# Second attention layer of a streaming encoder: where its cached keys are turned, and in which order two small products run

## The reference

```python
def fox_attend(q, k, v, cq, ck, qpos, kpos):
    s = jnp.einsum('bqhd,bkhd->bhqk', q, k) * (FOX_HEAD_DIM ** -0.5)
    s = s + swapaxes(cq, 1, 2)[:, :, :, None] - swapaxes(ck, 1, 2)[:, :, None, :]
    s = jnp.where(kpos[None, :] <= qpos[:, None], s, -jnp.inf)
    return jnp.einsum('bhqk,bkhd->bqhd', softmax(s, axis=-1), v)

def swiglu_ffn(x, w_in, w_out):
    a, u = jnp.split(x @ w_in, 2, axis=-1)
    return (jax.nn.silu(a) * u) @ w_out
```

## Time and profile before

| | |
|---|---|
| time of three runs, median (lowest to highest) | 1886.13 us (1880.18 to 1888.01) |
| profiled execution, span from first to last instruction | 1885.1 us |
| TensorE busy | 1849.9 us (98%) |
| VectorE, ScalarE, GpSimd busy | 983.0, 722.0, 225.9 us |
| HBM read, written | 243.19 MB, 13.19 MB |
| first and second attention steps | about 118 to 190 and 1487 to 1568 us |
| up product of the third layer's FFN | about 1105 to 1285 us |

### The profile page before, as it was taken

How to read it: one execution, slowest core, us unless ns; L and a number is a source line. 1 busy time by engine, 2 the same in 40 slices (tenths; PEclk the granted TensorE clock), 3 DMA queues, 4 the chain that set the end, 5 groups by cost and what they waited for, 6 DMA issues and landing times.

```text
span 1885.1 us, 29064 instructions
## 1 busy us (share of the span) xinstructions
PE 1849.9 (98%) x12004; PEld 1642.4 (87%) x12004; DVE 983.0 (52%) x1569; ACT 722.0 (38%) x1144; POOL 225.9 (12%) x357
## 2 busy tenths in 40 slices
PE   8999999999999999999999999999999999999998
PEld 8777799998888887799998899998897777999986
DVE  4557653443567778743443664443465576543434
ACT  4246443333255454333332343333242463433321
POOL 3114070000011222230000100000031230000000
PEclk9999999999999999999999999999999999999999
DMA  7357254433353433444433434433364562444332
GB/s 246 128 203 229 81 160 123 129 129 123 117 164 105 125 116 104 118 139 125 124 134 123 146 101 125 132 124 125 110 206 150 200 221 90 137 132 124 128 129 79
DMA packets 179171, 259.38 MB, mean 138 GB/s; under 512 B 14717, under 2 KB 122349, under 8 KB 179040
## 3 DMA queue, kind: packets, MB, share of 16 engines
q1 hardware_dynamic: 161184, 197.18, 32.3%
q0 software_dynamic: 17856, 60.35, 9.9%
HBM read 243.19 MB, written 13.19 MB: 136 GB/s over the span
## 4 chain that ended last, share of the span: by engine, by line
PE 90%; DVE 4%; ACT 3%; issue 1%; DMA 1%; SPq 0%; DVEq 0%; ACTq 0%
PE ps L1605 14%; PE ps L1607 14%; PE ps L1606 14%; PE ps L1617 11%; PE ps L1615 11%; PE ps L1616 11%; PE ps L1833 1%; PE ps L1951 1%; PE ps L1938 1%; PE ps L1638 1%; PE ps L1888 1%; PE ps L1671 1%; DVE w_lo L785 1%; PE ps L1908 1%; PE ps L1673 1%
## 5 line engine op out<-in xcount | busy, mean ns | idle before, releaser
L785 DVE TENSOR_TENSOR w_lo<-w_raw,w_hi 128x1024 fp32r<-128x1024 f32 x370 | 452.1, 1228 | 709.1 <-ACT w_hi L439 707.9
L439 ACT ACTIVATE w_hi<-w_raw 128x1024 fp32r<-128x1024 f32 x370 | 389.3, 1059 | 803.5 <-DMA w_raw<-in_w_ffn_in_dram 363.1
L1605 PE MATMUL ps<-xT_hi,w_hi 128*128 128x384 f32 x1568 | 528.4, 337 | 2.5 <-issue 1.4
L1607 PE MATMUL ps<-xT_hi,w_lo 128*128 128x384 f32 x1568 | 527.0, 336 | 0.0
L1606 PE MATMUL ps<-xT_lo,w_hi 128*128 128x384 f32 x1568 | 526.9, 336 | 0.0
L1605 PEld LDWEIGHTS ps<-xT_hi,w_hi 128*128 128x128 f32 x1568 | 294.8, 188 | 5.2 <-issue 5.1
L1606 PEld LDWEIGHTS ps<-xT_lo,w_hi 128*128 128x128 f32 x1568 | 294.8, 188 | 0.1
L1607 PEld LDWEIGHTS ps<-xT_hi,w_lo 128*128 128x128 f32 x1568 | 294.8, 188 | 0.0
L1617 PE MATMUL ps<-w_hi,hT_lo 128*128 128x512 f32 x528 | 210.6, 399 | 0.0
L1616 PE MATMUL ps<-w_lo,hT_hi 128*128 128x512 f32 x528 | 208.1, 394 | 0.0
L1615 PE MATMUL ps<-w_hi,hT_hi 128*128 128x512 f32 x528 | 207.4, 393 | 0.0
(11 more groups left out here) (329 smaller groups left out, 2021.8 us busy)
## 6 DMA issues: line engine op xcount, KB each, us to landing
w_raw<-in_w_ffn_in_dram SPq DMA_DIRECT2D x352, 256.0 KB, 3.2
w_raw<-in_w_ffn_out_dram SPq DMA_DIRECT2D x176, 256.0 KB, 2.9
w_raw<-in_w_fox_in_dram SPq DMA_DIRECT2D x96, 256.0 KB, 2.9
k_c<-in_cache_fox_k_dram POOLq DMA_DIRECT2D x32, 512.0 KB, 5.3
v_c<-in_cache_fox_v_dram POOLq DMA_DIRECT2D x32, 512.0 KB, 4.0
w_raw<-in_w_hgrn_in_dram SPq DMA_DIRECT2D x64, 256.0 KB, 2.9
w_raw<-in_w_fox_out_dram SPq DMA_DIRECT2D x32, 256.0 KB, 2.9
out_dram<-kv_tok POOLq DMA_DIRECT2D x4, 1024.0 KB, 5.0
```

The lines of the kernel that those rows point to most:

```text
L439: nc.scalar.activation(w_hi[:, slot, :], w_raw[:, slot, :], ACT.Copy).then_inc(hi_ready, 1)
L785: V.tensor_tensor(w_lo[:, slot, :], w_raw[:, slot, :], w_hi[:, slot, :].bitcast(F32), ALU.subtract).then_inc(lo_ready, 1)
L1605: mm(out, w_hi[:, slot, cols], x_hi[:, k, :], start=k == 0, stop=False, skip_group_check=True)
L1607: last = mm(out, w_lo[:, slot, cols], x_hi[:, k, :], start=False, stop=k == KD - 1, skip_group_check=True)
```

## The change

For the layer i = 3 (`AHEAD`) the cached keys are no longer turned by TensorE in the attention loop. In the FFN of layer 2, GpSimd loads them as `k_nat`, four streams and 256 columns at a time (1 MB in 1 KB pieces, `cached_keys`). VectorE turns them by eight transposes of 128x256 in blocks of 32x32, each writing every eighth word of `k_turn` (`turn_keys_ahead`, behind `hT_lo` of chunks 1 to 8). SP stores the result to a DRAM tensor `keys_t`, in four DMAs of 32 partitions (`store_turned`, behind the weight loads of chunks 3 to 10). In layer 3 SP loads `k_t` from it, 512 KB in 1 KB pieces for each half stream, three slots: the first three before the last projection chunk, the others in the loop, between the sixth and the seventh unit of the output product (`turned_keys`). GpSimd puts the 16 new keys into `k_t` (`new_keys`); SP's keys replace its `load_k`. `ktc`, L605, L928 and L929 are left out in this layer, and `s_keys` with them.

Also in layer 3 alone: the bias product goes ahead of `s_out` and of the pairs (`s_bias`, it starts the accumulation, the pairs end it); `s_fold` moves into the middle of `p_scores` and `p_out`; `folded_hi` on ScalarE goes behind the exponential and `folded_lo` on VectorE behind the scaling of the prompt's probabilities; and GpSimd's third `v_c` load waits for `c_lo`. Semaphores of other layers are used again. The core of the diff, in which `b0`, `cols` and the new memory places are cut:

```diff
@@ sync
+            def turned_keys(i, first, end):
+                f = FOX[i]
+                for n in range(first, end):
+                    b, hf = n // 2, n % 2
+                    if n < KV:
+                        sync.wait_ge(*at(KEYS["stored"], 64 * DB))
+                        sync.wait_ge(unit_used, START[i]["mix"])
+                    else:
+                        sync.wait_ge(*at(f["s_scores"], n - KV + 1))
+                    sync.dma_start(k_t[:, n % KV, :, 0:PAST], keys_t[b, hf * WCOLS:(hf + 1) * WCOLS, :].rearrange(
+                        "(g p) k -> p g k", p=P)).then_inc(KEYS[f"in{n % KV}"][0], 16)
+            def store_turned(n):
...
+                sync.wait_ge(*at(KEYS["turned"], n + 1))
+                for r in range(4):
+                    sync.dma_start(keys_t[b0 + r, cols, :].rearrange("(c d) k -> d c k", d=32),
+                                   k_turn[32 * r:32 * r + 32, :, :, :].rearrange("d c k a -> d c (k a)")).then_inc(KEYS["stored"][0], 16)
...
+                    if i == AHEAD:
+                        chunks(w_fox_in[j], s["mix"], 6, 0, 5 * CU)
+                        turned_keys(i, 0, KV)
+                        chunks(w_fox_in[j], s["mix"], 6, 5 * CU)
+                        chunks(w_fox_out[j], s["out"], 2, 0, RING)
+                        turned_keys(i, KV, 2 * DB)
+                        chunks(w_fox_out[j], s["out"], 2, RING)
...
+                    if i + 1 == AHEAD and 3 <= c < CF:
+                        store_turned(c - 3)
@@ scalar, fox
                     if 1 <= n <= HEADS:
                         act.wait_ge(*at(f["s_nmax"], n))
...
+                    if 2 <= n <= HEADS + 1 and i == AHEAD:
+                        folded_hi(n - 2)
+                    if 1 <= n <= HEADS:
                         act.wait_ge(*at(f["s_pT"], n))
...
-                    if 1 <= n < HEADS:
+                    if 1 <= n < HEADS and i != AHEAD:
                         act.wait_ge(*at(f["ktr"], n + 1))
@@ vector, ffn and fox
+                    if i + 1 == AHEAD and 1 <= c <= DB:
+                        turn_keys_ahead(c - 1)
+            def turn_keys_ahead(n):
+                dve.wait_ge(*at(KEYS["loaded"], 16 * (n + 1)))
+                if n:
+                    dve.wait_ge(*at(KEYS["stored"], 64 * n))
+                for a in range(TWIN):
+                    ins = V.transpose(k_turn[:, :, :, a], k_nat[:, a, :])
+                ins.then_inc(KEYS["turned"][0], 1)
...
                         ins.then_inc(f["scaled"][0], 1)
+                    if 2 <= n <= HEADS + 1 and i == AHEAD:
+                        folded_lo(n - 2)
...
-                        if n:
+                        if n and i != AHEAD:
                             key_sides(n, KT_BANKS + 1)
@@ gpsimd
+                if i == AHEAD:
+                    pool.wait_ge(*at(f["c_lo"], 3))
+                else:
+                    pool.wait_ge(unit_used, m0 + 12)
+                    load_k(KV - 1)
                 load_v(KV - 1)
...
+                    if n < 2 * DB and i == AHEAD:
+                        pool.wait_ge(*at(f["s_scores"], n - KV + 1))
+                        new_keys(n)
+                    elif n < 2 * DB:
                         pool.wait_ge(*at(f["ktr"], n - KV + 1))
                         load_k(n)
...
+            def cached_keys(i, j):
+                pool.wait_ge(unit_used, START[i - 1]["up"] + 2)
+                for n in range(DB):
...
+                    if n:
+                        pool.wait_ge(*at(KEYS["turned"], n))
+                    pool.dma_start(k_nat[:, :, :], cache_fox_k[j, b0:b0 + 4].rearrange("b (p a) h d -> (b p) a (h d)", a=TWIN)[
+                        :, :, cols]).then_inc(KEYS["loaded"][0], 16)
@@ tensor, fox
+                        if e and i == AHEAD and k:
+                            s_fold(2 * k - 2)
                         out = ps[:, S_BANK[e], 0:T]
...
                     for a in range(2):
+                        if a and i == AHEAD and k < KD - 1:
+                            s_fold(2 * k + 1)
...
+                def s_bias(n):
                     if n:
                         pe.wait_ge(*at(f["s_exp"], n))
+                    mm(ps[:, SS_BANK, 0:PAST + DT], sel_s[:, n % 2, :], c_s[:, n // 2, :], start=True, stop=False,
+                       skip_group_check=True)
...
+                    if i == AHEAD:
+                        pe.wait_ge(*at(KEYS[f"in{n % KV}"], 16 * (n // KV + 1)))
+                        pe.wait_ge(*at(KEYS["new"], n + 1))
...
+                    if n < HEADS and i == AHEAD:
+                        s_bias(n)
                     if n:
                         s_out(n - 1)
```

More of the change, by code:

```diff
@@ L72 @@
 LATE = 2
+AHEAD = 3
+TWIN = 8
+TCOLS = 256
 def phase_starts():
@@ L303, in trunk_program @@
         y_stored = sem("y_stored")
+        H = HGR[KINDS.index("hgrn")]
+        KEYS = {"loaded": (H["st0_in"][0], 16 * (HG // 2)), "stored": (x_in[0], 16),
+                "turned": (H["snew"][0], 2 * HG), "new": (H["gate"][0], 2 * GRP),
+                "in0": (x_in[1], 16), "in1": (x_in[2], 16), "in2": (turned_in, 0)}
         CT_AFTER, CT_BANK, CT_LF = (8, 9, 10, 11, 12), (7, 3, 7, 3, 7), 4
@@ L1338, in fox, with new_keys @@
                 assert laid == LAID
-                pool.wait_ge(unit_used, m0 + 12)
-                load_k(KV - 1)
+                if i == AHEAD:
+                    pool.wait_ge(*at(f["c_lo"], 3))
+                else:
+                    pool.wait_ge(unit_used, m0 + 12)
+                    load_k(KV - 1)
                 load_v(KV - 1)
                 pool.wait_ge(*at(f["laid"], LAID))
+                def new_keys(n):
+                    now = slice(SEQ + DT * (n // 2), SEQ + DT * (n // 2) + DT)
+                    G.tensor_copy(k_t[:, n % KV, :, PAST:], kT[:, 4 * (n % 2):4 * (n % 2) + 4, now]).then_inc(KEYS["new"][0], 1)
                 def store(n, marked, kp, ks):
@@ L1361, in fox @@
                 pool.wait_ge(*at(f["kT_a"], KD))
+                if i == AHEAD:
+                    for n in range(KV):
+                        new_keys(n)
                 pool.wait_ge(*at(f["kstored"], 16 * 2))
@@ L1969, in fox @@
                         p_scores(n // 2)
+                    if n == HEADS and i == AHEAD:
+                        s_fold(n - 2)
                     if n == 0:
```

94 lines of the change are left out of this document (57 added, 37 removed).

## The result

| | before | after |
|---|---|---|
| median (lowest to highest), us | 1885.43 (1880.18 to 1888.01), 4 runs | 1919.68 (1918.34 to 1920.16), 4 runs |
| profiled execution, span | 1885.1 | 1918.1 |

What follows compares the result with a forecast made beforehand. Attention steps were bound by a chain between engines (odd) or by TensorE (even). Steps save 9.1 and edges 1.5, taken as 10.5, with nothing lost elsewhere: 1885.1 - 10.5 + 1.0 = 1875.6 us, range 1868 to 1885.

Steps and rivals of the forecast that it cites:

- `s_out`, the pairs, the maximum and the exponential after the last `s_turn`: Second attention's steps: `s_out` starts 1.20 us after `s_turn` instead of 1.68, pairs 1.89 instead of 2.37, odd-step maximum at 2.64.
- Gaps 3.74 and 4.40: Second attention, between `s_turn` starts: odd steps 3.74 us instead of 4.54 (chain-bound), even steps 4.40 instead of 4.99 (TensorE-bound).
- 13 gaps: Second attention, seven odd and six even steps between `s_turn` at 1495.36 and 1557.03: 61.7 us, to save 9.1.
- I take 0, at most 2 us: Second attention: key loads on SP's queue, share 0.77, slots filled two to three steps ahead, cost 0, at most 2 us.
- Edges: Around the second attention's regular steps: first `s_keys` 0.87 us, step before 1495.36 at most 0.15, last 0.45; together 1.5.
- The transposes, 0.7 us each, 5.6 per chunk: VectorE in the third layer's up product: eight per chunk at 0.7 us, between 0.41 and 2.06, making 5.6 us.
- so the wait is hidden: Third layer's up product: SP's wait for transposes ends 9.7 us after a chunk's end, before the next weight slot at 12.4.
- Cost nothing.: Third layer's FFN: SP's stores put the next weights back by 0 to 6 us, against 15 of slack, at no cost.
- 15 us of room: Third layer's up product: VectorE's weight split is ready at 1157.5 and used near 1172.6, so may be 15 us late.
- The loads: Extra key traffic: DMA share 0.40 to about 0.8 in the FFN, stores landing in 6 us; attention share 0.77.
- The slower rival, 1915: Third layer's FFN: weight splits starve through long transposes or DMA share above 1; 1915 us at 2.06 per transpose; chance 0.12.
- the 1.22 us from which it decides: Third layer's up product: VectorE's 6.8 of 16.5 us per chunk leaves 9.7, or 1.22 us per transpose; beyond it splits starve.

Runs made afterwards that it cites:

- later stores: Changed kernel with SP issuing each piece's stores two units later, behind the next chunk's first two weight loads: 1878.84 us, 0.9971 of the kernel before.
- new values first: On top of later stores, GpSimd issues the second attention's 32 KB new-value load before the 512 KB cached values: 1873.48 us, 0.9942 of the kernel before.
- more transposes: On top of later stores, eight additional unused 128x160 transposes per chunk on VectorE: 1888.21 us (one run).
- the traffic alone: Changed kernel without transposes: same loads and stores, a zeroed buffer stored without waiting, the last layer's cached keys left out: 1878.62 us (one run).
- the bias back behind the pairs: On top of later stores, the second attention's bias product returns behind the pairs while the folds stay moved: 1883.18 us (one run).
- the silu first: Changed kernel, third layer's up product: silu ahead of two of four `w_hi` copies, transposes ahead of two `w_lo`; stores unmoved: 1879.12 us, 0.9967 of before.
- the keys alone: On top of later stores and new values first, bias product and folds both back at their old places: 1878.45 us, 0.9965 of the kernel before.

## Why the prediction was wrong, point by point

1. *`s_out`, the pairs, the maximum and the exponential after the last `s_turn`.* Predicted at T+1.20, 1.89, 2.64 and 3.11; in after at T+1.19, 1.77, 2.60 and 3.08 (T = 1557.48). Right.
2. *Gaps 3.74 and 4.40.* They are 3.79 and 4.33. The 13 gaps should have come to 52.6; they do in the version without DMA waits (52.51), and are 54.35 in after. The difference is the two waits for the new values. The prediction watched the key and the value loads ("I take 0, at most 2 us") and not the small DMA behind them in GpSimd's queue; the size was inside the 2 us.
3. *Edges.* First gap 0.15 shorter, as said (4.53 to 4.38 or 4.39); last gap 0.50 shorter for 0.45. The first `s_keys` (0.87) does not show in the stretch up to the first `s_turn` of after, which is longer by 1.2: TensorE has less to do there and waits for the first exponential, 1.18 us where it had been 0.40. Where the ring is cut by the later stores or by the new values first, that stretch is shorter by 0.8 and 0.4.
4. *The transposes, 0.7 us each, 5.6 per chunk.* 64 of them:

```profile
L978 DVE STREAM_TRANSPOSE k_turn<-k_nat x64: 607/644/727, 1138.4 to 1303.9; 128x256 f32<-128x256 f32 x64
```

   Choosing a value near the low end of 0.41 to 2.06 was right, though 5.6 us per chunk was too much: the durations overlap, and eight in a row take 3.96 us, 0.50 each. By the Trainium skill (Vector Engine (DVE) Microarchitecture Reference, section "Measured stream behaviour on trn2") the estimate had been 0.72 for an output that steps by non-adjacent words; the trace has 0.64 at the median and 0.73 at most for one, and 0.50 in a row, so the output's steps cost less here than by that estimate.
5. *"These end 4.1 (hT_lo done at 1156.1) plus 5.6, 9.7 us after a chunk's end; the next weight slot that SP could fill comes free after three units, at 12.4, so the wait is hidden"* and *"Cost nothing."* This is the step that failed, twice over.
   - The chunk's end was put at 1152.03, the start of silu. But silu stood behind a copy on ScalarE that had itself waited for a load:

```profile
1151.06 1.06 ACT L439 ACTIVATE w_hi<-w_raw 128x1024 fp32r<-128x1024 f32 x1 [2.82 <-DMA w_raw<-in_w_ffn_in_dram]
```

   That load can start only when the chunk's last unit is done and its slot free. So the chunk ended a load's issue and landing (about 0.7 and 3.2 us) and a copy (1.0) before silu, near 1147.2, 4.8 us earlier than taken. With the silu moved ahead of that copy, the stretch from the last silu to the first `s_turn` is 210.2 us instead of the 205.5 and 205.9 of the two versions with later stores: silu starts 4.3 to 4.7 earlier against the rest. With this, 4.8 + 4.0 + 4.0 + 3.3 = 16.1 us pass from a chunk's end to the last store's issue, against 12.4: not hidden.
   - Missing these 4 us would have cost little once (an estimate; no run has the delay without the ring). But the load for which silu waits stands behind the stores in SP's queue: the wait was costed as a delay that ends, and it was an edge of a ring that feeds on its own lateness. I had asked who is queued behind SP's wait and when that unit's `w_lo` is due on TensorE (15 us of room), and not who else waits for its `w_hi`: the silu, by nothing but its place on ScalarE.
6. *The loads.* Share 0.8 forecast, 0.74 to 0.75 where TensorE runs through, stores landing at 6.1 for the 6 taken: right. In the attention 0.66 (1535 to 1600) for 0.77, and no wait for keys or cached values. Weight loads that landed in 3.2 us need 7.0 in after and 4.3 with later stores and new values first. Without the ring TensorE does not wait for them; in the ring the 3.8 us more of landing are part of each 23.2.
7. *The slower rival, 1915.* Its time was near the measured 1919.7, its cause was not there: the transposes are half of the 1.22 us from which it decides, and the DMA share in that product stays at 0.60. Splits that starve behind the transposes do appear where GpSimd issues the stores and with more transposes, for 5.5 and 7.4 us, by a wait for a buffer and not by the transposes' length alone. No rival had the order of SP's queue as its mechanism.

Without the failed step the prediction holds: the version with later stores comes out 3.2 us above the forecast of 1875.6, that with the new values first 2.1 below. How near a median comes is in part luck, as they are 5.6 and 11.3 us below the runs of before taken with them. The stages say it better: from the first silu of the third layer's up product to the end the profiled executions take 754.3 and 753.2 us for 763.3 before, 9.0 and 10.1 less, where 10.5 was forecast.

## What to carry to other kernels

A wait put between the prefetches of an in-order DMA queue is not paid when it ends but when the prefetch behind it lands: follow that prefetch to every instruction that stands behind its consumer on each engine, and if one of these leads back to what is being waited for, the period is the sum around the ring, however idle the engines are. Put loads that the next round needs in front of stores that this round makes; here two places in SP's queue were worth 40 us. Moving the stores to another queue only moves the question: there they stood in front of the load of `k_nat`, and made a smaller ring. And take as the end of a stage the last instruction of the engine that does it, not the first of the one that follows: the follower may be late for a reason of its own.

## What the chip showed that I had not expected

- Landing time does not follow the mean share. At a share of 0.60 the 256 KB weight loads take 7.0 us instead of 3.2 at 0.40. At 0.74 to 0.77, spread more evenly, they take 4.3 to 4.9 in the versions with later stores, 5.6 with the traffic alone and 6.2 with more transposes. In after the traffic comes in bursts (each digit is the busy share of one of 40 slices of 1140 to 1290, in tenths):

```profile
DMA  3999700899800699900599910399930199950099
```

- A 32 KB DMA issued behind a 512 KB one on the same queue lands in 4.8 us, ahead of it in 2.4. In the kernel before, behind such a one too, it was 3.3.
- A wait of TensorE in the attention costs more than its length where the clock falls behind it. The two waits of 1.1 us in after lengthened their gaps by 0.9 us each and left the clock at 1.00. With the bias back behind the pairs, one wait of 2.3 us (at 1500.85) was followed by a granted clock of 0.55, near the lower of its two levels, and the gap is 3.9 us longer than its kind, the next 0.8:

```profile
1494.00:1501.00 7.00, 4.36 (x60) 2.66 (x61) 2.65 (x11) 4.32 (x16) 1.49 (x3) 1.00 0.94 330
1501.30:1506.00 4.70, 4.70 (x40) 2.99 (x31) 1.97 (x7) 0.69 (x3) 1.49 (x3) 0.55 0.63 216
1506.00:1512.00 6.00, 5.77 (x57) 3.81 (x55) 2.92 (x12) 2.97 (x11) 1.49 (x3) 0.79 0.32 88
```

  So was the wait of 1.6 us in the run with the silu first: 0.66 from 1525 to 1530, and a gap of 7.33 for 4.33. The wait's length does not decide it alone: with the keys alone, a wait of 1.15 us in front of the first `s_turn` was followed by 0.79 over the next 8 us and the gap of 6.09, while with the new values first the same wait, 1.18 us, was followed by 1.00. Unlike in the ring of the FFN, TensorE is what the next steps wait for here.
- A transpose of 128x256 words in 32x32 blocks with outputs 32 bytes apart takes 644 ns in after and 710 in the run with more transposes, one of 128x160 there 503. They overlap: eight in a row take 3.96, 4.3 and 2.75 us, so 0.50, 0.54 and 0.34 us each.
